# Residual kept in DRAM during the experts, a ring of twenty weight units, and another order of sums at the end of the last layer

## The reference, cut to what matters

```python
for i in range(DEPTH):
    h = modulate(rms_norm(x, norm_mix[i]), sh_m, sc_m)
    x = x + g_m * mixer_i(h)
    h = modulate(rms_norm(x, norm_ffn[i]), sh_f, sc_f)
    x = x + g_f * hier_moe(h, ...)       # sum over two experts: combine * (silu(h@w1) * (h@w3)) @ w2
return x
```

## Time and profile before

| what | value |
|---|---|
| median of 3 runs | 1156.07 us (1155.21 to 1157.74) |
| the profiled execution's own time | 1158.26 us |
| its span | 1156.5 us |
| granted TensorE clock, mean | 0.976 |
| HBM read, written | 316.71 MB, 33.05 MB |
| busy: TensorE, VectorE, ScalarE, GpSimd | 1040.6, 610.6, 327.8, 95.6 us |
| experts of layer 0, of layer 1 | about 355 to 592 us, about 897 to 1152 us |

### The profile page before, as it was taken

One profiled execution on the slowest core, in us unless ns is written; L12 is line 12 of the kernel. 1 busy time (PEld: TensorE's weight loads), 2 busy tenths in 40 slices (PEclk: granted clock), 3 DMA queues, 4 the chain that ended last, 5 costly groups with the idle time before them and its releaser, 6 DMA issues.

```text
span 1156.5 us, 15189 instructions
## 1 busy us (share of the span) xinstructions
PE 1040.6 (90%) x5622; PEld 629.6 (54%) x5622; DVE 610.6 (53%) x1457; ACT 327.8 (28%) x894; POOL 95.6 (8%) x124
## 2 busy tenths in 40 slices
PE   4999999899997999887879999899999999979985
PEld 2444444555466566554546665555457766646552
DVE  6899988885666422222246477767235622222225
ACT  4321122874231211111124455566112121111110
POOL 1000000000001111111000000000000111101102
PEclk9999999999998999899999999999998999999998
DMA  9929869008977999999995300200915699999996
GB/s 368 394 95 418 332 229 368 33 1 354 410 289 296 398 418 419 418 420 419 420 380 229 122 1 20 91 1 26 412 55 236 248 421 418 419 420 419 419 418 268
DMA packets 63790, 333.05 MB, mean 288 GB/s; under 512 B 10774, under 2 KB 11030, under 8 KB 32864
## 3 DMA queue, kind: packets, MB, share of 16 engines
q1 hardware_dynamic: 48080, 293.49, 62.6%
q0 software_dynamic: 13968, 33.44, 7.5%
q10 hardware_dynamic: 1664, 5.09, 1.1%
HBM read 316.71 MB, written 33.05 MB: 302 GB/s over the span
## 4 chain that ended last, share of the span: by engine, by line
PE 69%; DMA 15%; DVE 5%; SPq 5%; ACT 3%; issue 3%; DVEq 0%; POOLq 0%; ACTq 0%
PE PP L639 12%; PE PP L845 11%; PE PP L753 10%; DMA AHS<-in_moe_w 6%; PE PP L860 6%; DMA ring<-in_moe_w 5%; SPq L501 5%; PE PP L990 3%; PE PP L661 3%; DMA RQK<-in_moe_w 3%; PE PP L1032 3%; PE PP L612 2%; PE PP L1036 2%; PE PP L648 2%; PE PP L698 2%
## 5 line engine op out<-in xcount | busy, mean ns | idle before, releaser
L639 PE MATMUL PP<-ring,AHS 128*128 128x512 f32 x320 | 139.9, 593 | 0.0
L1887 DVE TENSOR_TENSOR PS<-PS,PP 128x256 f32<-128x256 f32 x33 | 13.9, 421 | 204.9 <-PE PP L845 195.6
L753 PE MATMUL PP<-ring,AHS 128*128 128x512 f32 x256 | 111.3, 594 | 1.4 <-ACT AHS L1362 0.8
L1894 DVE SCALAR_TENSOR_TENSOR PS<-PP,small,GF 128x512 f32<-128x512 f32 x66 | 46.5, 746 | 110.0 <-PE PP L860 101.5
L845 PE MATMUL PP<-RQK,RV 128*64 128x256 f32 x768 | 91.0, 396 | 14.8 <-issue 11.7
L639 PEld LDWEIGHTS PP<-ring,AHS 128*128 128x128 f32 x320 | 59.8, 190 | 69.7 <-issue 69.7
L845 PEld LDWEIGHTS PP<-RQK,RV 128*64 128x64 f32 x768 | 66.9, 143 | 41.9 <-issue 25.7
L845 PE MATMUL PP<-ring,RV 128*64 128x256 f32 (+1 forms) x672 | 80.2, 382 | 7.4 <-issue 3.9
L753 PEld LDWEIGHTS PP<-ring,AHS 128*128 128x128 f32 x256 | 48.2, 190 | 59.6 <-issue 59.6
L845 PEld LDWEIGHTS PP<-ring,RV 128*64 128x64 f32 (+1 forms) x672 | 60.8, 141 | 29.5 <-issue 10.1
L845 PE MATMUL PP<-AHS,RV 128*64 128x256 f32 x640 | 71.8, 380 | 3.9 <-issue 3.9
(11 more groups left out here) (342 smaller groups left out, 1636.1 us busy)
## 6 DMA issues: line engine op xcount, KB each, us to landing
RQK<-in_moe_w SPq DMA_DIRECT2D x68, 1024.0 KB, 21.7
ring<-in_moe_w SPq DMA_DIRECT2D x63, 1024.0 KB, 24.2
AHS<-in_moe_w SPq DMA_DIRECT2D x60, 1024.0 KB, 27.1
ring<-in_ada_t SPq DMA_DIRECT2D x22, 1024.0 KB, 8.4
AHS<-in_ada_t SPq DMA_DIRECT2D x18, 1024.0 KB, 7.5
ring<-in_da_w_qkv SPq DMA_DIRECT2D x10, 1024.0 KB, 11.1
RQK<-in_ada_t SPq DMA_DIRECT2D x8, 1024.0 KB, 10.6
y_d<-GF POOLq DMA_DIRECT2D x2, 4096.0 KB, 37.8
```

The lines of the kernel that those rows point to most:

```text
L639: last = mm(PB[qkv_bank(n)][:, :], HT[:, c, t * P:(t + 1) * P], us[c // 4][:, (c % 4) * NH:(c % 4 + 1) * NH], start=c == 0, stop=c == C - 1)
L753: last = mm(PB[2 * t + n][:, :], (OT, OTM)[l][:, k, t * P:(t + 1) * P], us[k // 2][:, (k % 2) * D + n * NH:(k % 2) * D + (n + 1) * NH], st ...
L1894: last = stt(ysb[b][:, cols], PB[5 + m][:, :], weight, GF[:, cols], ALU.mult, ALU.mult)
```

## The change

What it does:

- A second copy of X is stored to a new DRAM tensor `kept_d` by GpSimd's queue, tile by tile behind the stores of `xn_d`, in both layers. During the experts the memory of X is free, and becomes two more slots (18 and 19) of the ring.
- The ring is one sequence of twenty slots. Unit u of a layer (u = 6n + k) takes place u mod 20 of `slot_order`, and from unit 20 on waits for the product that read unit u - 20. The order of places is: the ring slots that hold no output projection weights, two that do, AHS slots 16, 17, 12 to 15, the RQK slots, the remaining two held ring slots, the two X slots.
- SP's list for the first units is written anew. It now waits for the first two gathers of a layer to land before the units 16 to 19 (layer 0) or 18 and 19 (layer 1) and everything behind them.
- Reading X back: in layer 0 tile 0 when the w1 product of pair 13 is done, ahead of Y of tile 0, and tiles 1 to 3 each ahead of its Y; in layer 1 all four tiles on SP's queue behind the last weights.
- The end of layer 1: the mixing products of the four tiles go to eight PSUM banks; the rows k = 1 of the tiles 1 to 3 are added in the same banks by TensorE (a product with the identity), and GpSimd's three sums are gone. VectorE starts with a wait for all four tiles of X, adds the row k = 0 (for tile 0 both rows), then the banks. The last tile is stored in two halves.
- The semaphores of SP's and GpSimd's turns are merged into one; the functions of the old order go away.

The core of the diff:

```diff
+SLOTS = BANKS * RING + 2
+END_BANKS = (2, 3), (4, 7), (0, 1), (5, 6)
+X_SLOT = BANKS * RING
...
+        kept_d = [nc.dram_tensor(f"kept_d{l}", [S, D], F32) for l in range(2)]
...
+            if s >= X_SLOT:
+                return X[:, 2 * (s - X_SLOT):2 * (s - X_SLOT) + 2, :].rearrange("p t n -> p (t n)")
...
+            unheld = [r for r in range(RING) if not holder[r] or holder[r][0] != "wo"]
+            held = [r for r in range(RING) if r not in unheld]
+            slot_order.append(unheld + held[:2] + [16, 17, 12, 13, 14, 15] + list(range(RING, 2 * RING)) + held[2:] + [18, 19])
+            for u in range(6 * PAIRS):
+                slot = slot_order[l][u % SLOTS]
+                fills[slot] += 1
+                arrival[l][("moe", *divmod(u, 6))] = (slot, 16 * fills[slot])
...
+        in_x_slot = len([u for u in range(6 * PAIRS) if u % SLOTS == X_SLOT])
+        for t in range(T):
+            own = in_x_slot if t < 2 else 0
+            loaded["rows", t] = 16 * (1 + own + 2)
+            loaded["mla", t] = loaded["rows", t] + 16
+            loaded["last rows", t] = loaded["mla", t] + 16 * (own + 1)
...
                     if l == 1 and n == 0:
+                        sp.wait_ge(sem("a"), LAST - 1)
+                        load_x(kept_d[0], 0)
                         sp.wait_ge(sem("rows"), 1)
                         for b in range(2):
                             sp.wait_ge(sem(f"scat{b}"), 16 * SCATS[b])
                         sp.dma_start(Y[0], y_rows[0][0]).then_inc(sem("xl0"), 16)
                     if l == 1 and n == 3:
                         for t in range(1, T):
+                            load_x(kept_d[0], t)
                             sp.dma_start(Y[t], y_rows[0][t]).then_inc(sem(f"xl{t}"), 16)
...
+            def free_at_first(l, slot):
+
+                if slot < RING:
+                    if moe_holder[l][slot]:
...
+                    sp.wait_ge(*((sem("omla"), 8) if l else (sem("oe"), 8)))
                 else:
-                    sp.wait_ge(*((sem("omla"), 8) if l else (sem("oe"), 8)))
+                    sp.wait_ge(sem("kept_out"), 16 * T * (l + 1))
...
+            def expert_unit(l, u):
+
+                n, k = divmod(u, 6)
+                slot = arrival[l][("moe", n, k)][0]
+                if u < SLOTS:
+                    free_at_first(l, slot)
+                else:
+                    before, part = divmod(u - SLOTS, 6)
+                    sp.wait_ge(sem("aby"[part // 2]), PAIRS * l + before + 1)
+                sp.dma_start(unit(slot), (w1, w3, w2)[k // 2][l][n + PAIRS * (k % 2)]).then_inc(s_w[slot], 16)
...
-                projecting = [k for k in range(6) if moe_holder[l][(first_slot[l] + k) % RING][0] == "wo"]
-                experts(l, 0, range(6 if l else 4))
-                experts(l, 1, [k for k in range(6) if k not in projecting])
-                experts(l, 2, (0, 1, 4, 5) if l else (4, 5))
                 if l == 0:
+                    for u in (0, 1, 10, 11, 12, 13, 4, 5):
+                        expert_unit(0, u)
                     for entry in late:
                         load_unit(*entry)
-                    experts(0, 0, (4, 5))
-                experts(l, 1, projecting)
-                experts(l, 2, (2, 3) if l else (0, 1, 2, 3))
-                for n in range(BANKS, BETWEEN):
+                    for u in (14, 15, 2, 3, 6, 7, 8, 9):
+                        expert_unit(0, u)
+                else:
+                    for u in (0, 1, 10, 11, 12, 13, 14, 15, 4, 5, 6, 7, 2, 3, 16, 17, 8, 9):
+                        expert_unit(1, u)
+                for b in range(2):
+                    sp.wait_ge(sem(f"gath{b}"), 16 * (PAIRS // 2 * l + 1))
+                for u in (18, 19) if l else (16, 17, 18, 19):
+                    expert_unit(l, u)
+                experts(l, BANKS, (2, 3, 4, 5))
+                for n in range(BANKS + 1, BETWEEN):
...
+            sp.wait_ge(sem("a"), PAIRS + LAST - 1)
             for t in range(T):
-                sp.wait_ge(sem("res"), 2 * T + t + 1)
-                sp.dma_start(out[t * P:(t + 1) * P, :], X[:, t, :]).then_inc(sem("out"), 16)
-            sp.wait_ge(sem("out"), 16 * T)
+                sp.dma_start(X[:, t, :], kept_d[1][t * P:(t + 1) * P, :]).then_inc(sem("out"), 16)
+            for t in range(T):
+                rows = slice(t * P, (t + 1) * P)
+                if t < T - 1:
+                    sp.wait_ge(sem("res"), 2 * T + 2 * t + 2)
+                    sp.dma_start(out[rows, :], X[:, t, :]).then_inc(sem("out"), 16)
+                else:
+                    for m in range(2):
+                        cols = slice(m * NH, (m + 1) * NH)
+                        sp.wait_ge(sem("res"), 2 * T + 2 * t + m + 1)
+                        sp.dma_start(out[rows, cols], X[:, t, cols]).then_inc(sem("out"), 16)
+            sp.wait_ge(sem("out"), 16 * (2 * T + 1))
...
+            def second_rows(t):
+
+                pe.wait_ge(sem(f"xl{t}"), loaded["last rows", t])
+                for m in range(2):
+                    last = mm(PB[END_BANKS[t][m]][:, :], ident[:, :], Y[t][:, 1, m * NH:(m + 1) * NH], start=False, stop=True)
+                last.then_inc(sem("mix"), 1)
+
+            def mix_at_end():
+
+                pe.wait_ge(sem("yD"), 2 * PAIRS)
+                mix(hot_last, LAST % 2, 0, END_BANKS[0]).then_inc(sem("mix"), 1)
+                mix(hot_last, LAST % 2, 1, END_BANKS[1], alone=False)
+                mix(hot_last, LAST % 2, 2, END_BANKS[2], alone=False)
+                second_rows(1)
+                mix(hot_last, LAST % 2, 3, END_BANKS[3], alone=False)
+                second_rows(2)
+                second_rows(3)
...
+            def add_at_end():
+
+                dve.wait_ge(sem("out"), 16 * T)
+                for t in range(T):
+                    dve.wait_ge(sem(f"xl{t}"), loaded["last rows", t])
+                    for k in range(2 if t == 0 else 1):
+                        link(tt(X[:, t], X[:, t], Y[t][:, k], ALU.add))
+                    dve.wait_ge(sem("mix"), T + t + 1)
+                    for m in range(2):
+                        cols = slice(m * NH, (m + 1) * NH)
+                        tt(X[:, t, cols], X[:, t, cols], PB[END_BANKS[t][m]][:, :], ALU.add).then_inc(sem("res"), 1)
...
                     pool.wait_ge(sem("xn"), 4 * (2 * l + 1) + t)
                     pool.dma_start(xn_d[l][t * P:(t + 1) * P, :], XN[:, t, :]).then_inc(sem("xd"), 16)
+                    pool.dma_start(kept_d[l][t * P:(t + 1) * P, :], X[:, t, :]).then_inc(sem("kept_out"), 16)
...
-                for t in range(1, T if l else 0):
-                    pool.wait_ge(sem(f"xl{t}"), 64)
-                    g.tensor_tensor(Y[t][:, 0], Y[t][:, 0], Y[t][:, 1], ALU.add).then_inc(sem("ysum"), 1)
```

More of the change, by code:

```diff
@@ L409, in build @@
         streams = ring_plan(A)
-        plan, arrival, fills, holder = [], [{}, {}], [0] * (BANKS * RING), [None] * (BANKS * RING)
+        plan, arrival, fills, holder = [], [{}, {}], [0] * SLOTS, [None] * X_SLOT
         holder[RING + 4] = ("dat", 16)
-        first_slot, moe_holder = [], []
+        slot_order, moe_holder = [], []
+        loaded = {}
+        fills[X_SLOT:] = [1, 1]
         for l in range(2):
-            now, last_slot = [], 0
+            now = []
             for key, src, k, slot, free in streams[l]:
@@ L436, in stored @@
         def stored(l, n):
-            turn = first_slot[l] if n % BANKS == RING_BANK else 0
-            return lambda k: bank[n % BANKS][:, (turn + k) % RING, :]
+            return lambda k: unit(arrival[l][("moe", n, k)][0])
         block = enter(nc.Block())
@@ L470, in stream @@
                     load_unit(*entry)
-            def free_scores(l, k):
-                sp.wait_ge(sem("sc"), 32 * (l + 1))
-                if l == 0 and k >= 4:
-                    sp.wait_ge(sem("ada"), 48)
-            def free_ring(l, k):
-                name, value = moe_holder[l][(first_slot[l] + k) % RING]
-                sp.wait_ge(sem(name), value)
-            def free_projected(l, k):
-                if k < 2:
+            def free_at_first(l, slot):
+                if slot < RING:
+                    if moe_holder[l][slot]:
+                        sp.wait_ge(sem(moe_holder[l][slot][0]), moe_holder[l][slot][1])
+                elif slot < 2 * RING:
+                    sp.wait_ge(sem("sc"), 32 * (l + 1))
+                    if l == 0 and slot >= RING + 4:
+                        sp.wait_ge(sem("ada"), 48)
+                elif slot < 2 * RING + 2:
@@ L508, in last_experts @@
                     for k in (4, 5):
-                        sp.wait_ge(sem("y"), PAIRS * l + LAST - BANKS + 1)
+                        before, part = divmod(6 * LAST + k - SLOTS, 6)
+                        sp.wait_ge(sem("aby"[part // 2]), PAIRS * l + before + 1)
                         cols = slice(c * D, (c + 1) * D)
@@ L966, in experts @@
                     expert_step(l, n)
-                for t in range(T if l else 0):
```

(19 more changed lines are left out.)

60 lines of the change are left out of this document (23 added, 37 removed).

## The result

The changed kernel takes 1152.02 us in the median of 10 runs where the kernel before takes 1156.62: ratio 0.9948, 95% interval 0.9932 to 0.9963, so 6.0 us less (4.3 to 7.9; the two medians differ by 4.6). The forecast was 4.9 less. The profiled execution has a span of 1150.8 us against 1156.5, 5.7 less. The total came out close because errors of opposite sign met, and the stages show them.

A forecast was written before the change was run, and what follows sets the result against it. The weight stream on the DMA engines was taken to bound the expert phases; -2.1 (layer 0), -3.9 (layer 1), +0.8 (hand-over) and +0.3 (end) sum to -4.9 us, a median of 1151.2, range 1147.5 to 1158.0.

The forecast's parts named there:

- What bounds it: Both expert phases: the full weight stream sets the end, so gains lie where DMA engines idled ahead of it.
- Layer 0, forecast -2.1: Start of layer 0's weight stream: gathers land near 362.4, unit 18's data start 2.3 us earlier; 2.1 us gained, 0.2 to 3.5.
- less 0.6 and plus 0.4: Layer 0's stream: the third gather now shares it, costing 0.6 us; a small DMA hole closes, gaining 0.4.
- Layer 1, forecast -3.9: Start of layer 1's weight stream: units 18 and 19 issued at 903.6, data 3.7 us earlier; 3.9 us gained, 2 to 4.7.
- The hand-over, forecast +0.8: Between the layers: X read ahead of Y rows costs 0.3 us for tile 0, 0.5 for tile 2; 0 to 2.5.
- The end, forecast +0.3: After the last rows: TensorE's 28 instructions, smaller last store, X ahead of Y rows; 0.3 us lost, -0.6 to +5.
- the freed slots: Expert phases: twenty slots let loads wait for an earlier product, but the stream is already at its rate; nothing gained.
- GpSimd's longer queue: Eight residual stores on GpSimd's queue: issues of about 0.55 us each are covered; only 1.25 us of data counted, in layer 0.
- The gate that opens no earlier: Rival, layer 0: gathers share DMA engines evenly, so fewer units behind them don't help; layer 0 gives 0.2, 1153.1, chance 0.15.
- The slower rival: Both hand-overs: reading X back lies on the path, up to 5.0 us at each; +4.0, 1160.1 us, chance 0.14.

The follow-up runs named there:

- rows after modulation: Changed kernel with the third projection unit loaded behind X and Y of tile 1, and tile 2's rows added after tile 1's modulation; ratio 0.9922 to the kernel before.
- two units held: Changed kernel, but in layer 0 SP holds back only units 18 and 19 for the first gathers, not 16 to 19; ratio 0.9948 to the kernel before.

## Why the prediction was right, and where it was not

**What bounds it.** Right: both gains lie where the DMA engines had holes. The holes are smaller, not gone: the idle time from 355 to 385 us was 8.6 us and is about 3.

**Layer 0, forecast -2.1, measured -4.4.** The mechanism was right, the term too small. The step was the second gather's landing, "between 361.0 and 364.3; I take 362.4". It landed at 359.5, 6.1 us after the first gather's issue and not 7.4. The queue drained at 358.0, not 360.4: 0.7 us because its last unit was issued earlier, and 1.7 because that unit landed 15.5 us after its issue, where 21.0 less two units and plus the residual's copy makes 17.25. A cost of 1.25 us for the copy does not show in this. And the gathers were down 1.5 us behind the drain, not 2. With the gate at 6.1 the forecast's own way gives 3.6 for the earlier start, less 0.6 and plus 0.4, so 3.4; the other 1.0 is open. The first product also came earlier (365.4 instead of 369.7), but with four units held and twenty slots the stage follows the gate and not the product. With eighteen slots the earlier product is what brings the next unit forward, and the forecast did not see that this alone gives 3.3 to 4.6.

**Layer 1, forecast -3.9, measured -3.1** (1.8 to 3.3 less in the six other runs that keep gate and slots). The gate opened at 901.74, 6.1 us after the first gather's issue, as forecast. I took the slots for the cause and did not see the gate's share: without it the same slots gave 0.2 us in the one trace there is, 1.7 us of the loss being the hole behind the overflow tile, which may be partly the clock's. So the gate's share lies between about 1.2 and 2.9. Against eighteen slots with the first product late by the clock (242.8, 242.5) the slots without the gate are 1.7 to 2.0 better.

**The hand-over, forecast +0.8, measured +2.6.** The step that failed is the reading of which Y tile is late. I priced tiles 0 and 2 and left out tile 1. Y of tile 1 is issued at 583.48 and lands 15.8 us later, at 599.3, where VectorE was ready at 596.8. Ahead of it stand X of tile 0 and of tile 1. In the kernel before it landed 12.2 us after its issue at 589.2, at 601.4, and VectorE took it at 602.65, a slack of 1.2 us. By my own price of 1.25 us for each X the loss would have been 1.3; they cost 3.6 us of landing, 1.8 each, as in the run that reads tile 1 twice. So the tile was left out, and the price was low as well. Tile 2 was then on time, because its demand had moved back with tile 1's. The bound up to 2.5 for this term was passed by 0.1. And the difference understates the loss: against the same hand-over without the waits (18.7 us, rows after modulation) it is 4.3, since the stage of the kernel before was itself long by a low clock in its first projection (8.30 us, and 5.40 at a clock of 1.00).

**The end, forecast +0.3, measured -0.7.** The walk through TensorE's 28 instructions was right in kind (14.3 us forecast from the last rows to VectorE's end, 14.7 measured, TensorE late ahead of tile 2's sum by 0.65). The late Y rows were priced at 3.1 us, and tile 0's adds waited 3.0. What was off is the span behind VectorE's last add, 2.5 us instead of 4.1, where I had 0.6 less: the half store gave 0.5, and 1.0 behind its landing was not foreseen.

**Nothing for the freed slots and for GpSimd's longer queue:** nothing in the traces contradicts it. The last copy of layer 0 was down at 350.9, not near 348.5, still ahead of the gate. The stores were tried by themselves, without a decision; the freed slots were not. They have a price that the forecast left out: with twenty slots the stream can stand at the overflow tile, 1.7 us of idle in the trace without the gate.

**The rivals.** The gate that opens no earlier is refuted by its opening at 359.5, 6.1 us after the first gather's issue, where it opens after 10.4 us with two units held. By the Trainium skill ("DMA: Bandwidth & Descriptors", arbitration) the engines take packets from their queues in turn. The runs show that this does not make a gather independent of the weights ahead: 8.8 us with two units held, 3.7 to 5.8 with four. The slower rival had the right place, and its price was 2.6 and 0.3 us (16.9 to 17.25 at the end) rather than 5.0 at each.

## What to carry to other kernels

Ahead of a stream that then runs full, look for what starts it: here two small gathers waited behind megabytes that nobody needed yet, and in layer 0 holding those back gave as much as the extra memory did (3.3 to 4.6 us and 2.9), for one wait, and the two together less than their sum. A load that is put in front of others is paid by the first consumer without slack, so walk every consumer in order, not the one that looks latest. When a wait moves instead of going, change the order in which the results are wanted.

## What was not expected of the hardware

- Two gathers of 128 rows land 3.7 to 5.8 us after their issue when the weights ahead of them have drained or nearly so, and 6.8 to 10.7 us when they have not, although they are on another queue.
- VectorE's adds beside GpSimd's sums took up to 3.33 us for 1.22 alone.
- The granted clock around the routing changes from run to run, and with eighteen slots a dip there moves the first product by 1.6 to 2.5 us and the whole stage of layer 1 with it. With the gate the stream begins with the gathers, and of the seven traces with gate and twenty slots six lay between 237.7 and 238.3, one at 239.1. In three of the six the first product was just as late (11.3 us after the gather), in the one at 239.1 12.1.
